# Projection prologue of an encoder layer: where squares are kept, one inverse tile per block, an early third load, tile order

## The reference

```
h = RMSNorm(x)            # x * rsqrt(mean(x^2) + eps) * norm_mix
p = h @ W_in              # one projection into all the branches' inputs
# branch A: RWKV-7 time mixing over shifted r, k, v and low-rank decay, rate and gate
# branch B: GLU -> depthwise convolution of width 31 -> LayerNorm -> swish
# x = x + (sigmoid(gA) * A + sigmoid(gB) * B) @ W_out
# x = x + ExpertChoiceSwiGLU(RMSNorm(x));  final RMSNorm
```

## Time and profile before

| | us |
|---|---|
| median of 3 runs | 2488.1 |
| lowest, highest | 2484.7, 2490.22 |
| the profiled execution's own time | 2486.42 |
| its span | 2484.6 |
| TensorE (PE) busy | 2329.5 (94%) |
| VectorE (DVE) busy | 1823.7 (73%) |
| ScalarE (ACT) busy | 1211.8 (49%) |
| GpSimd (POOL) busy | 722.4 (29%) |

### The profile page before, as it was taken

One profiled execution on the slowest core, in us unless ns is written; L12 is line 12 of the kernel. 1 busy time (PEld: TensorE's weight loads), 2 busy tenths in 40 slices (PEclk: granted clock), 3 DMA queues, 4 the chain that ended last, 5 costly groups with the idle time before them and its releaser, 6 DMA issues. The chain is left out here.

```text
span 2484.6 us, 50105 instructions
## 1 busy us (share of the span) xinstructions
PE 2329.5 (94%) x19520; PEld 2034.6 (82%) x19520; DVE 1823.7 (73%) x2475; ACT 1211.8 (49%) x1751; POOL 722.4 (29%) x721
## 2 busy tenths in 40 slices
PE   6899999999998999987999995799999999999997
PEld 3688888888887999985766674799999999999996
DVE  4547888988895676674767677677777777777777
ACT  5355444544522334433334332665656666666556
POOL 2233243442422444464454535011111111101111
PEclk9999999999998999998999997899999999999998
DMA  4325243352566766763647352877777777777777
GB/s 153 86 88 163 92 158 115 114 174 73 169 206 187 208 190 192 194 169 109 222 128 253 111 198 99 322 256 260 261 246 239 251 259 254 246 252 266 261 254 245
DMA packets 294772, 479.74 MB, mean 193 GB/s; under 512 B 142224, under 2 KB 209952, under 8 KB 266832
## 3 DMA queue, kind: packets, MB, share of 16 engines
q1 hardware_dynamic: 275552, 412.52, 50.5%
q0 software_dynamic: 7760, 27.08, 4.9%
q10 hardware_dynamic: 11296, 37.82, 4.7%
HBM read 363.51 MB, written 110.69 MB: 191 GB/s over the span
## 5 line engine op out<-in xcount | busy, mean ns | idle before, releaser
L2975 PE MATMUL bank<-e_xt,e_w_high 128*128 128x384 f32 x1792 | 525.3, 357 | 3.5 <-DVE e_xt L3143 2.2
L3130 DVE TENSOR_TENSOR e_w_low<-e_w,e_w_high 128x2048 fp32r<-128x2048 f32 x192 | 436.4, 2286 | 69.3 <-ACT e_w_high L3031 69.3
L2976 PE MATMUL bank<-e_xt,e_w_low 128*128 128x192 f32 x1792 | 449.3, 251 | 0.0
L3031 ACT ACTIVATE e_w_high<-e_w 128x2048 fp32r<-128x2048 f32 x192 | 366.5, 1909 | 108.0 <-PE bank L2997 79.3
L2976 PEld LDWEIGHTS bank<-e_xt,e_w_low 128*128 128x128 f32 x1792 | 342.5, 191 | 0.6
L2975 PEld LDWEIGHTS bank<-e_xt,e_w_high 128*128 128x128 f32 x1792 | 338.2, 189 | 5.3 <-issue 2.5
L712 PE MATMUL bank<-h_high,w_high 128*128 128x512 f32 x864 | 259.3, 408 | 1.2 <-DVE work L1158 1.2
L1141 DVE SCALAR_TENSOR_TENSOR work<-work,vec 128x1551 f32<-128x1551 f32 x116 | 243.2, 2096 | 2.2
L715 PE MATMUL bank<-h_low,w_high 128*128 128x512 f32 x864 | 244.2, 391 | 0.0
L718 PE MATMUL bank<-h_high,w_low 128*128 128x512 f32 x864 | 243.5, 390 | 0.0
L2909 POOL DMA_INDIRECT xacc_dram<-e_y,e_put x30 | 47.3, 1577 | 648.3 <-DVE e_y L3165 643.8
(11 more groups left out here) (385 smaller groups left out, 5119.0 us busy)
## 6 DMA issues: line engine op xcount, KB each, us to landing
e_w<-in_ew SPq DMA_DIRECT2D x192, 1024.0 KB, 5.3
features_dram<-work SPq DMA_DIRECT2D x48, 512.0 KB, 3.3
front<-features_dram SPq DMA_DIRECT2D x24, 1024.0 KB, 6.1
x_w<-in_w_mix SPq DMA_DIRECT2D x48, 512.0 KB, 4.8
w<-in_w_in ACTq DMA_DIRECT2D x35, 512.0 KB, 3.6
ba_tok_dram<-work SPq DMA_DIRECT2D x96, 128.0 KB, 2.4
gates_dram<-work ACTq DMA_DIRECT2D x16, 768.0 KB, 4.6
all<-ba_tok_dram SPq DMA_DIRECT2D x56, 128.0 KB, 3.3
```

The lines of the kernel that those rows point to most:

```text
L2975: nc.tensor.matmul(*wide, start=(k == 0), stop=False)
L2976: nc.tensor.matmul(*narrow, start=False, stop=False)
L3031: nc.scalar.activation(w_high[n % RING][:], w[n % RING][:], ACT.Copy).then_inc(w_high_done, 1)
L3130: tt(w_low[n % RING][:], w[n % RING][:], w_high[n % RING][:].bitcast(F32), ALU.subtract)\
```

## The change

- The squares of block 1 move to the first half of `front`, those of block 2 to the second; `inv` becomes a tile per block, those of blocks 1 and 2 in the part conv. `root(b)` no longer waits for the scaling of the block before.
- SyncE issues the load of block 2 of x right behind that of weight 1, with no wait for the sums.
- ScalarE's order: root(0) goes ahead of the squares of block 1; the high parts of a block are cut in groups, with high(1) or squares of the next block between them; root(2) goes ahead of `up_parts`. `squares(2)` no longer waits for the sums of block 0.
- VectorE no longer folds the squares of block 2; TensorE sums them with four matmuls a half, as for block 1, and waits for the Ln of root(0) instead of its Exp.
- TensorE multiplies blocks 0 and 1 in tile order too, and waits for the weights of tile 1 only at tile 1.
- GpSimd makes `h_rest(0)` ahead of `low(1)`.

```diff
-        inv, k_first = spare, spare
+        k_first = spare
+        inv = [spare] + [conv[:, b * BLK:(b + 1) * BLK] for b in range(NB - 1)]
...
-        square = [halves(2 * (NB if b != 1 else 2)) for b in range(NB)]
+        square = [halves(work, 2 * NB), halves(g.front, 0), halves(g.front, 2)]
...
             load(1)
-            sp.wait_ge(summed, 4)
             for h in range(2):
                 load_x(2, h)
...
                 if b >= 2:
-                    pe.wait_ge(rooted, b - 1)
-                paired = b != 1
+                    pe.wait_ge(logged, b - 1)
+                paired = b == 0
...
-            for b in range(NB - 1):
-                for k in range(KD):
-                    split_in(b, k)
-                    for t in range(2):
-                        if b == 0 and k == 0:
-                            pe.wait_ge(w_split, t + 1)
-                        first(t, b, k)
+            for b in range(NB):
+                for t in range(2):
+                    if b == 0:
+                        pe.wait_ge(w_split, t + 1)
+                    for k in range(KD):
+                        if t == 0:
+                            split_in(b, k)
+                        mm = first(t, b, k)
+                    if b == NB - 1:
+                        mm.then_inc(projected, 1)
                 if b == 0:
                     sums(2)
...
             low(0)
+            h_rest(0)
             low(1)
-            h_rest(0)
             h_rest(1)
...
             def root(b):
                 act.wait_ge(summed, 2 * b + 2)
-                act.wait_ge(normed, KD * b)
...
             squares(0, 0)
             squares(0, 1)
             high(0)
+            root(0)
             squares(1, 0)
-            root(0)
             squares(1, 1)
+            h_top(0, 0, 2)
             high(1)
-            h_top(0)
+            h_top(0, 2, 4)
+            root(1)
             squares(2, 0)
+            h_top(1, 0, 2)
             squares(2, 1)
-            root(1)
-            h_top(1)
+            h_top(1, 2, 4)
+            root(2)
             act.wait_ge(up_in, 16)
             nc.scalar.activation(up_parts[:], up, ACT.Copy).then_inc(up_split, 1)
-            root(2)
-            h_top(2)
+            h_top(2, 0, 4)
...
             for b in range(NB):
                 dve.wait_ge(rooted, b + 1)
-                if b == 1:
-                    fold(2)
                 scale(b, range(0, 4))
```

More of the change, by code:

```diff
@@ L509, in project @@
         x = [work[:, b * KD * BLK:(b + 1) * KD * BLK].rearrange("p (k t) -> p k t", k=KD) for b in range(NB)]
-        halves = lambda at: [work[:, (at + h) * 4 * BLK:(at + h + 1) * 4 * BLK].rearrange("p (k t) -> p k t", k=4)
-                             for h in range(2)]
-        square = [halves(2 * (NB if b != 1 else 2)) for b in range(NB)]
+        halves = lambda v, at: [v[:, (at + h) * 4 * BLK:(at + h + 1) * 4 * BLK].rearrange("p (k t) -> p k t", k=4)
+                                for h in range(2)]
+        square = [halves(work, 2 * NB), halves(g.front, 0), halves(g.front, 2)]
         x_in = [[sem("p_x_in00"), sem("p_x_in01")]] + [2 * [sem(f"p_x_in{b}")] for b in range(1, NB)]
@@ L890, in squares @@
                 act.wait_ge(x_in[b][h], 16 if b == 0 else 32)
-                if b == 2:
-                    act.wait_ge(summed, h + 1)
                 nc.scalar.activation(square[b][h], x[b][:, 4 * h:4 * h + 4, :], ACT.Square).then_inc(squared, 1)
@@ L896, in root, with h_top @@
                 act.wait_ge(summed, 2 * b + 2)
-                act.wait_ge(normed, KD * b)
-                nc.scalar.activation(inv, g.bank[6 + b % 2][:], ACT.Ln, bias=g.c("eps", 0, 1),
+                nc.scalar.activation(inv[b], g.bank[6 + b % 2][:], ACT.Ln, bias=g.c("eps", 0, 1),
                                      scale=1.0 / D).then_inc(logged, 1)
                 act.wait_ge(logged, b + 1)
-                nc.scalar.activation(inv, inv, ACT.Exp, scale=-0.5).then_inc(rooted, 1)
-            def h_top(b):
-                for n in range(4):
+                nc.scalar.activation(inv[b], inv[b], ACT.Exp, scale=-0.5).then_inc(rooted, 1)
+            def h_top(b, lo, hi):
+                for n in range(lo, hi):
                     act.wait_ge(normed, KD * b + 2 * n + 2)
@@ L1092, in scale @@
                 for k in ks:
-                    stt(x[b][:, k, :], x[b][:, k, :], g.v("norm_mix", k), inv, ALU.mult, ALU.mult).then_inc(normed, 1)
+                    stt(x[b][:, k, :], x[b][:, k, :], g.v("norm_mix", k), inv[b], ALU.mult, ALU.mult).then_inc(normed, 1)
             fold(0)
```

## The result

The changed kernel takes 2476.97 us (median of 7 runs, 2468.95 to 2481.23) where the kernel before takes 2489.22 (7 runs, 2483.64 to 2491.53): ratio 0.995, 95% interval 0.9931 to 0.997. That is 12.3 us; the interval reaches from 7.5 to 17. The forecast was 14.7 us and 2473.5, with a range of 2467 to 2482.

What follows compares the result with a forecast made beforehand. TensorE, busy throughout from 125.5 to 640 us, was taken as the bound. Reaching the key sums 12.9 us sooner, plus 1.8 for no slow stretch behind the wait, gave 14.7 off the median: 2473.5 us, range 2467 to 2482.

Steps and rivals of the forecast that it cites:

- Scaling of the blocks: VectorE's prologue: block 0 at 18.75 us (was 23.35), block 1 at 34.4 (was 46.5), block 2 at 50.3 (was 62.03).
- The idle time ahead of tile 2: TensorE before tile 2: idle some 3.4 us (1.2 before), costing a stretch at 1.2 GHz, 1.8 us.
- The two ways through the key sums: TensorE: after a slow stretch arrives at 111.6 without waiting, gain 14.7; at full clock waits 1.2 until 111.0, gain 15.3.
- The table loads: ScalarE at roots 0 and 2: loads hidden because they do not wait for data; otherwise 1.3 us more at each.
- The memset: VectorE's tail, now beside GpSimd's low part: could cost from nothing to 2.0 us; taken as nothing.
- rival 2: VectorE's memset waits for GpSimd, tail 2.0 us longer: gain 12.6 us, 2475.5; chance 0.15.
- the sums of block 1: TensorE's prologue: 16 records from 20.5 us with one 3.4 us stretch at 1.2 GHz, ending 29.4, then block 0's products.
- w_low of tile 1: GpSimd's low part of tile 1's weights: takes 2.4 us, ends about 34.8, asked for at 34.9; hidden, just.
- a sign of being wrong: TensorE in block 0: waiting for w_low or h_low there would show the forecast wrong; no size given.
- Rival 1: Prologue: TensorE at 1.2 GHz in block 1's sums (+4.8) or table loads not hidden (+2.6); gain say 10, 2478; chance 0.12.
- Rival 3: Behind the key sums: gains given back in later stages, leaving a gain within 5 us, 2485; chance 0.08.
- rival 4: Dense TensorE stretch from 29 to 69 us runs at 1.2 GHz: up to 25 us slower, 2513; chance 0.03.

Runs made afterwards that it cites:

- E12: The changed kernel itself, run again unedited beside its variants: median 2476.43 us (6 runs), ratio 0.9951 to the kernel before.
- E8: Changed kernel plus throwaway TensorE filler products around block 0's sums, ahead of block 1's sums and ahead of tile 2: median 2477.91 us, ratio 0.9956.
- E2: Changed kernel with root 0 behind both squares of block 1 again: tile 0 shifted at 78.39 us, 5.5 us late.
- E10: Changed kernel with the edits of E6 and E7 together, and eight of sixteen duplicating DMAs issued from ScalarE's queue: median 2472.36 us, ratio 0.9938.
- E6: Changed kernel with memset, one low part and ScalarE's copy of up_parts moved ahead of block 2's scaling: tile 0 shifted at 70.53 us, 2.3 us sooner.
- E5: Changed kernel with block 2's squares folded by VectorE again, between its scalings of block 1: tile 0 shifted at 75.29 us for 72.86.
- E1: Changed kernel with blocks 0 and 1 multiplied slice by slice again, each for tiles 0 and 1: tile 0 shifted at 80.1 us (corrected) for 72.86.
- E4: Changed kernel with block 2's load issued after block 1's sums again: 2484.14 us, timed once; tile 0 shifted 0.6 us late (corrected).
- E7: Changed kernel with ScalarE's tanh of the low-rank tile ahead of the next weight's high part: tanh at 73.5 us (corrected), 0.8 us sooner.
- E3: Changed kernel with one shared inverse tile and the wait for the previous block's scaling: 2470.64 us, timed once; tile 0 shifted at 72.72 us.

## Why the prediction was right, and where it was off

*The steps.* Scaling of the blocks was forecast at 18.75, 34.4 and 50.3 and measured at 18.89, 34.41 and 50.32; the sums of block 2 from 40.4, measured 40.58; tile 2 at 72.8, measured 73.00; tanh at 74.0, measured 74.22. The idle time ahead of tile 2 was forecast at 3.4 us and measured 3.06. The two ways through the key sums are both seen: in the first profile at full clock, a wait of 1.25 and 111.25 (forecast 1.2 and 111.0), in E12 with a slow stretch, no wait and 112.20 (forecast 111.6).

*The table loads* are hidden at roots 0 and 2, as taken. *The memset* took 1.38 us at 67.53 beside GpSimd's instruction of 67.11 to 69.51, as long as in the earlier trace rows where it stood alone. So rival 2 is out. That is what the Trainium skill ("SBUF — State Buffer", section "Who interferes with whom") says of an instruction of VectorE that reads no more than one SBUF operand.

*The wrong path: the sums of block 1.* Their size was right (to 29.4, measured 29.35), but I put them, and one slow stretch in them, on the path, and priced w_low of tile 1 as hidden, just. E8 made the sums 1.6 us faster for nothing at block 2, and E2 showed that the split of block 0 and with it root 0 sets the pace; when the sums are slow for longer (E12), 0.9 us shows. Two chains end within a microsecond of each other at 35 us, and I summed along the wrong one. That the number came out right is luck: both chains agree. Within the other chain two errors cancel. I had w_low of tile 1 start at 32.5 and take 2.4 us; it started at 31.55 and took 3.39, beside VectorE's split, and ended at 34.94. TensorE did wait for it, by 0.18 us, which I had named as a sign of being wrong; it is that sign, at a size that costs next to nothing.

*Missing: the sums of block 0.* Before, 3.4 us lay between their end at 15.94 and the end of block 1's first square at 19.29 (17.38 + 1.91), and then came a table load that is no longer in the way. Now root 0 waits for them directly, and in three of the profiles their second half took 1.8 us more. The change put the first matmuls of the kernel on the path.

*The size in the median.* The time was forecast at 2473.5 and measured at 2476.97, inside the range of 2467 to 2482. The first profile gains 14.9 us by the end of the projection and E12 14.1, against a forecast of 14.7, while the medians say 12.3 and 13.5. Both lie within the interval. From the end of the projection to the end of the span the kernel before took 1725.0, the changed kernel 1722.5 and 1724.1 and E10 1730.3 us, without an edit there. The mean granted clock of E10 over the 400 us from 1081 was 0.95, against 0.97 before (400 us from 1100) and 0.96 in the changed kernel (400 us from 1085). I take the difference of medians for this spread. That is argued from these few profiles and not shown by a run of its own; a small amount given back later can't be told from it.

*Rivals.* Rival 1 in its own terms did not come: block 1's sums took 10.13 us at most (E10), not the 13.7 of 16 slow records, and the table loads were hidden; the slow sums of block 0 in some executions act like it. Rival 3 is excluded up to 744 us; rival 4 is out: where TensorE was dense from 29 to 69 us the clock stayed at 2.4 GHz in the first profile.

*Parts of the change.* By what undoing one costs at tile 0's shift: tile order 7.2 us (with the wait it causes and the clock it loses), root 0's place 5.5, no fold 2.4, early load 0.6, inverse per block 0. They overlap and are not to be summed. up_parts behind root 2 by itself wasn't run apart from E6; there ScalarE's copy fitted ahead of root 2 at no more than 0.6 us. GpSimd's order and the way the high parts are cut in groups weren't undone at all.

## What to carry to other kernels

When a prologue is a chain over several engines, write down for each join which two chains meet and how far apart they end; below a microsecond either may set the pace, and speeding up one of them gives nothing (E8, at the sums of block 2). Moving work to another engine can pay though both are on the path, when it costs less there: the unhalved sums held root 2 by 1.87 us, and the folds in their place made block 2 2.4 us later still (E5). A gain of half a per cent is better read at marks in the profile, some at the edit and one at the end of the stage, than from medians that spread by as much.

## What the runs showed of the hardware

- Idle time of TensorE and the clock: after 4.52 us ahead of block 1's sums (3.41 in E2) these took 8.59 to 10.13 us in every profile of the changed kernel and its variants without filler, for 7.13 with it (E8). After some 3.06 us ahead of tile 2 the clock fell in E1, E2, E4, E7 and E12 and stayed at 2.4 GHz in the changed kernel's first profile and E3. After 2.76 us in E6 it stayed; before, after 2.75 us at 65.95, it fell. The same kernel shows both.
- The first matmuls of a kernel ran at half speed: 3.75 us for the first four records against 1.95 when five filler products had gone before (E8). PEclk reads 1.00 over them, so this column does not show it. In E1, E4 and E7 the next four took 3.78 us as well, in the other profiles 1.98.
- A VectorE memset beside a GpSimd instruction took 1.38 us, as long as alone. VectorE's split, which has two inputs in SBUF, took 2.2 us where a GpSimd instruction was under way and 1.22 where none was; GpSimd's low part of tile 1's weights, begun while a split ran, took 3.39 us where that of a later weight took 2.40.
- Copies from SBUF to SBUF, 16 of 192 KB, ran at 226 to 246 GB/s with one issuing queue (the changed kernel) and 232 to 272 with two (E10), both from 80 to 90 us and with the 16 DMA engines at a busy share of 1.02 to 1.05. From tanh's end to the copy behind them they took 18.2 to 20.0 us with one queue and 18.5 with two.
